# Token columns of the projection matmuls: 512 + 512 + 128 instead of three times 384

## The reference

```
xn = rms_norm(x)
q, k, v, o, ig, fg, glu, xq, gates = split(xn @ w_in)
y_ml = mLSTM(q, k, v, ig, fg) * sigmoid(o)
y_cv = silu(layer_norm(causal_dwconv(ga * sigmoid(gb))))
y_xa = mem_attention(xq, mk, mv)
mixed = sum over b of sigmoid(gates[b]) * (y_b @ w_branch[b])
x = x + rms_norm(mixed @ w_out)
x = x + rms_norm((silu(fa) * fb) @ w_ffn_out)     # fa, fb from rms_norm(x) @ w_ffn_in
```

## Time and profile before

| | |
|---|---|
| median of three runs | 2942.29 us |
| span of the profiled execution | 2940.9 us |
| TensorE busy | 2737.7 us (93%), 15764 matmuls |
| weight loads busy | 2676.4 us (91%) |
| VectorE, GpSimd, ScalarE busy | 1066.5, 1043.4, 791.7 us |
| mean granted TensorE clock | 0.970 |
| projection units | 80, from about 130 to 1140 us |
| branch units | 24, in three groups |

### The profile page before, as it was taken

The page is one execution under the profiler, slowest core; times in us unless marked ns, Lnnn a source line. Parts: engine busy times, 40 slices in busy tenths (PEclk is TensorE's granted clock), DMA queues, the critical chain, the costliest instruction groups (busy, mean ns, idle before and its releaser), DMA issues.

```text
span 2940.9 us, 41651 instructions
## 1 busy us (share of the span) xinstructions
PE 2737.7 (93%) x15764; PEld 2676.4 (91%) x15764; DVE 1066.5 (36%) x1418; ACT 791.7 (27%) x1172; POOL 1043.4 (35%) x525
## 2 busy tenths in 40 slices
PE   5899999999999998989988989779998899969997
PEld 5899999999999998978788879769997899969997
DVE  3320399999922222156433423231103211041101
ACT  4321111111113323044311410233333333233332
POOL 5411222222211112122011201346665566646664
PEclk9999999999999999999999989989999899989999
DMA  6422333433252232534654435424444244433442
GB/s 174 139 88 92 121 118 112 136 115 108 91 178 89 82 96 100 168 106 117 210 174 167 148 133 187 156 76 123 137 141 136 86 121 139 132 115 114 124 134 78
DMA packets 469265, 372.11 MB, mean 127 GB/s; under 512 B 13626, under 2 KB 437906, under 8 KB 469168
## 3 DMA queue, kind: packets, MB, share of 16 engines
q1 hardware_dynamic: 454264, 317.52, 35.7%
q10 hardware_dynamic: 14912, 53.48, 4.7%
HBM read 285.86 MB, written 85.55 MB: 126 GB/s over the span
## 4 chain that ended last, share of the span: by engine, by line
issue 47%; PE 34%; POOL 14%; DVE 2%; ACT 1%; POOLq 1%; DMA 1%; SPq 0%; DVEq 0%; ACTq 0%
PE PS L274 29%; POOL w_lo L266 12%; PE PS L1504 1%; PE PS L1523 1%; PE PS L1179 1%; PE PS L1187 1%; PE PS L1145 1%; POOL m_lo L1776 1%; DVE x_T L549 0%; POOL m_lo L1987 0%; PE PS L1152 0%; DMA stage<-in_state_conv 0%; DVE y_T L1342 0%; POOL n_r L1971 0%; PE PS L1140 0%
## 5 line engine op out<-in xcount | busy, mean ns | idle before, releaser
L266 POOL TENSOR_TENSOR w_lo<-w_raw,w_hi 128x1024 fp32r<-128x1024 f32 (+1 forms) x324 | 838.1, 2588 | 1434.0 <-ACT w_hi L262 1433.9
L262 ACT CAST w_hi<-w_raw 128x1024 fp32r<-128x1024 f32 (+1 forms) x324 | 356.0, 1099 | 1755.5 <-PE PS L274 1749.0
L274 PE MATMUL PS<-A_hi,w_hi 128*128 128x384 f32 x3024 | 752.4, 336 | 19.0 <-DVE A_lo L948 10.0
L274 PE MATMUL PS<-A_lo,w_hi 128*128 128x384 f32 x3024 | 747.8, 335 | 0.0
L274 PE MATMUL PS<-A_hi,w_lo 128*128 128x384 f32 x3024 | 747.4, 335 | 0.0
L274 PEld LDWEIGHTS PS<-A_hi,w_hi 128*128 128x128 f32 x3024 | 546.2, 189 | 22.9 <-issue 18.0
L274 PEld LDWEIGHTS PS<-A_lo,w_hi 128*128 128x128 f32 x3024 | 546.2, 188 | 0.0
L274 PEld LDWEIGHTS PS<-A_hi,w_lo 128*128 128x128 f32 x3024 | 545.8, 188 | 0.0
L274 PE MATMUL PS<-m_hi,w_hi 128*128 128x384 f32 x1248 | 428.1, 343 | 28.1 <-DVE m_lo L1776 14.9
L274 PE MATMUL PS<-m_lo,w_hi 128*128 128x384 f32 x1248 | 425.7, 341 | 0.0
L274 PE MATMUL PS<-m_hi,w_lo 128*128 128x384 f32 x1248 | 425.4, 341 | 0.0
(11 more groups left out here) (265 smaller groups left out, 2103.5 us busy)
## 6 DMA issues: line engine op xcount, KB each, us to landing
w_raw<-in_w_ffn_in SPq DMA_DIRECT2D x132, 512.0 KB, 3.8
proj_d<-stage ACTq DMA_DIRECT2D x80, 576.0 KB, 2.8
w_raw<-in_w_in SPq DMA_DIRECT2D x80, 512.0 KB, 4.0
w_raw<-in_w_ffn_out SPq DMA_DIRECT2D x48, 704.0 KB, 4.6
gate_in<-proj_d SPq DMA_DIRECT2D x24, 576.0 KB, 6.2
part_d<-part_out SPq DMA_DIRECT2D x24, 576.0 KB, 4.5
w_raw<-in_w_branch SPq DMA_DIRECT2D x24, 512.0 KB, 4.2
w_raw<-in_w_out SPq DMA_DIRECT2D x24, 512.0 KB, 4.0
```

The lines of the kernel that those rows point to most:

```text
L262: nc.scalar.copy(w_hi[:, s % SPLIT, 0:kt], w_raw[:, s, 0:kt]).then_inc(w_hi_done, 1)
L266: nc.gpsimd.tensor_tensor(w_lo[:, s % SPLIT, 0:kt], w_raw[:, s, 0:kt], w_hi[:, s % SPLIT, 0:kt].bitcast(F32), ALU.subtract).then_inc(w_lo_ ...
L274: last = nc.tensor.matmul(out, w[:, k], m(k, c), start=start and k == 0 and n == 0, stop=stop and k == kt - 1 and n == 2)
```

## The change

The 1152 token columns of a unit go as 512, 512 and 128 columns instead of three times 384. The first two pieces fill a bank each, the third takes a quarter of one. As the pieces now lie without a gap across the three banks, the instructions that read them see one row of 1152 (`bank_rows`) instead of three pieces. In the first branch unit the waits for the low parts follow the new pieces: piece 0 (tokens 0 to 511) needs the first and the middle third, pieces 1 and 2 need all three. The FFN, the layer norm and the output projection keep their thirds of 384.

```diff
-                    nc.scalar.activation(thirds(stage[:, s % 2]), PS[:, 3 * (s % 2):3 * (s % 2) + 3, 0:TC], func,
+                    nc.scalar.activation(stage[:, s % 2], bank_rows(s % 2), func,
                                          scale=scale).then_inc(p_copied, 1)
...
         def a_hi(k, c):
-            return A_hi[:, k, TC * c:TC * (c + 1)]
+            return A_hi[:, k, 512 * c:min(512 * (c + 1), NTOK)]
 
         def a_lo(k, c):
-            return A_lo[:, k, TC * c:TC * (c + 1)]
+            return A_lo[:, k, 512 * c:min(512 * (c + 1), NTOK)]
 
         def banks(b):
-            return [PS[:, 3 * b + c, 0:TC] for c in range(3)]
+            return [PS[:, 3 * b], PS[:, 3 * b + 1], PS[:, 3 * b + 2, 0:NTOK - 1024]]
+
+        def bank_rows(b, p=slice(0, P)):
+            return PS[p, 3 * b:3 * b + 3].rearrange("p n c -> p (n c)")[:, 0:NTOK]
...
-            steps.mark(nc.vector.tensor_scalar(thirds(g_i[:]), PS[0:H, 3:6, 0:TC], g_bias[0:H, 0:1], None, ALU.add))
+            steps.mark(nc.vector.tensor_scalar(g_i[:], bank_rows(1, slice(0, H)), g_bias[0:H, 0:1], None, ALU.add))
...
                         for c in range(3):
-                            pe.wait_ge((ln_lo, ln_lo_pool, ln_lo)[c], (1, 1, 2)[c])
+                            pe.wait_ge(ln_lo, 1 if c == 0 else 2)
+                            pe.wait_ge(ln_lo_pool, 1)
...
-                    nc.vector.scalar_tensor_tensor(out=thirds(part_out[:, s % 2]), in0=thirds(gate_in[:, s % 2]), scalar=1.0,
-                                                   in1=PS[:, 3 * (s % 2):3 * (s % 2) + 3, 0:TC], op0=ALU.add,
+                    nc.vector.scalar_tensor_tensor(out=part_out[:, s % 2], in0=gate_in[:, s % 2], scalar=1.0,
+                                                   in1=bank_rows(s % 2), op0=ALU.add,
                                                    op1=ALU.mult).then_inc(part_mul if n else part_done, 1)
```

More of the change, by code:

```diff
@@ L829, in dve_proj @@
             dve.wait_ge(wif_used, 1)
-            steps.mark(nc.vector.tensor_scalar(thirds(g_i[:]), PS[0:H, 3:6, 0:TC], g_bias[0:H, 0:1], None, ALU.add))
-            nc.vector.tensor_scalar(thirds(g_f[:]), PS[32:32 + H, 3:6, 0:TC], g_bias[32:32 + H, 0:1], None, ALU.add).then_inc(gate_read, 1)
+            steps.mark(nc.vector.tensor_scalar(g_i[:], bank_rows(1, slice(0, H)), g_bias[0:H, 0:1], None, ALU.add))
+            nc.vector.tensor_scalar(g_f[:], bank_rows(1, slice(32, 32 + H)), g_bias[32:32 + H, 0:1], None, ALU.add).then_inc(gate_read, 1)
             dve.wait_ge(gate_read, 1)
```

## The result

The changed kernel takes 3092.7 us (median of 4 runs, 3087.1 to 3094.6) against 2942.5; the ratio is 1.0505, 95% interval 1.0491 to 1.0518. It is 5% slower. The forecast was 3100 us, within 3010 to 3140.

A forecast was written before the change was run, and what follows sets the result against it. TensorE was taken as the bound, busy for 93% of the span. 2520 triples at +60.0 ns (151.2 us) plus 6.6 us for the later branch start give +157.8 us on 2942.3: 3100 us, range 3010 to 3140.

The forecast's parts named there:

- The count and the place: Projection, branch and gate products: 2520 triples (three matmuls passing 1152 tokens by one weight piece), +60.0 ns each on TensorE, +151.2 us.
- The 128-column matmul: Third piece of a triple: its columns end before the next weights can load, so 113.3 ns; bounds 57.8 and 223.
- The 512-column matmul: First two pieces: 233.3 ns, stepping 60.0 ns per 128 columns from 256 (113.3) and 384 (173.3); bounds 216 and 240.
- (a): Smaller extra per 512: 226.7 ns with constant 13.3 ns, 3067 us (chance 0.22); or 216 ns, 3013 us (0.10).
- the unit of 13.9 us: Projection: ScalarE's evacuations, one per unit of 72 matmuls, would stand 13.9 us apart instead of 12.48.
- a 128 that is followed after less than 100 ns: In a triple: the next matmul starting under 100 ns after the 128 would make the prediction wrong; 113 expected.
- The start of the branch product: First branch matmul also waits for GpSimd's third of the low parts: start moves from 1149.23 to about 1155.8, +6.6 us.
- (b): Faster: next weights load ahead of the 128's start, 128 costs 57.8 ns, 512 costs 216; 2877 us, chance 0.05.
- (c): No change: matmuls cost by columns alone, triple stays 520.0 ns, only the later branch start counts; 2949 us, chance 0.04.
- (d): 128-column matmul falls into a slow form, 223 ns instead of 113.3; 3377 us, chance 0.06.
- (e): Pauses after each 128 lower the granted clock from 1.00 to 0.93 in the projection; 3210 us, chance 0.03.
- The formula from the Trainium skill: Warm matmuls take columns over 2.4 GHz plus 2.5 ns; triple 487.5 ns, so the change would gain, nearly as (b).

The follow-up runs named there:

- half_weights: Changed kernel, but the first 512-token matmul uses only 64 of 128 weight columns, so only the load after the 128-column matmul is shorter: 2938.8 us, 0.9984 of the kernel before.
- before_half_weights: Kernel before (three times 384) with 64 of the 128 weight columns on all three pieces in projection and branch units: 2946.2 us, 1.0008 of the kernel before.
- four_pieces: Pieces of 320 + 320 + 256 + 256 columns (first product of a unit: one 512 for the last two) instead of three times 384: 2976.8 us, 1.0112.
- wait_only: Kernel before (three times 384) with only the changed kernel's two wait lines in the first branch unit: 2949.4 us, 1.0024 of the kernel before.

## Why the prediction was right

**The count and the place**: 2520 triples, all on TensorE. (577 - 520) x 2520 + 6.6 = 150 us against 149.4 measured. The stage of the FFN kept its work: TensorE is busy for 1053.36 us in the last 1150 us of the span, 1053.64 before.

**The 128-column matmul**: taken at 113.3 ns, measured at 111 in a row and 108 in a triple, from load to load: 0.06 us to the listed start of the next 512 and some 0.05 of waiting. That the wait is the load's is shown by half_weights (gone with a load half as long) and before_half_weights (no effect where nothing is exposed). The exposed part is about 50 ns a triple, beside a loss of 57 against three times 384. (The 0.1115 us of a plain float32 matmul of 128 columns is 0.1117 by its row; nothing hangs on it.)

**The 512-column matmul**: taken at 233.3 ns by going on with 60 ns for each 128 columns. In a row it is 226.6, so the constant addition of rival (a) was right there; in the triple the two take 236 and 233. The result agrees, the argument doesn't hold. By its step 320 columns should take 143 ns, and they take 147 to 150; four_pieces should take 513 ns and takes 533, which the constant gives. The step came from the 113.3 ns of 256 columns; in the experiments a 256 takes 117 to 124, and the trace of the kernel before has another pace as well, in 4 of the 16 units of the memory tokens:

```profile
107.80 0.28 PE L274 MATMUL PS<-mem_hi,w_lo 128*128 128x256 f32 x1
...
110.27 0.28 PE L274 MATMUL PS<-mem_hi,w_lo 128*128 128x256 f32 x1
```

These are 21 periods, 117.6 ns each, at the same granted clock of 1.00 as in the stretch of the earlier trace rows; the step from them would have been 56 ns. So the mechanism of the 128 was right, and that the 512 had the right size in this mixture is luck. The forecast's 157.8 us are more than the measured 149.4 because the 128 was put 5 ns too high and the two 512s together 2 ns too low, and because the units from 56 on take 573 ns a triple.

**The signs**: the unit of 13.9 us came out (13.85), and so did the load that starts with the 128. The listed starts did not. They lie 0.28, 0.23 and 0.06 us apart, not 233, 233 and 113 ns, and by its letter the sign "a 128 that is followed after less than 100 ns" spoke against the prediction. The sign took the listed start for the beginning of the columns; read from load to load, the three are 236, 233 and 108 ns.

**The start of the branch product**: +6.6 us forecast, 6.66 in the trace (16.63 after 9.97), 6.5 by wait_only.

**The rivals**: (b) would need the load to begin ahead of the 128; it begins with it, at 400.87. (c) and (d) fall with the 108 to 111 ns, (e) with the granted clock of 1.00. The formula from the Trainium skill, "TensorE: Matmul & The Clock Gate", section "Back-to-back issue gap", gave an estimate of 487.5 ns a triple; the section itself offers it for a single matmul by itself and says that it counts too little for short ones in a stream of weight loads and matmuls, which the prediction did not say. The trace does not agree with the formula: 226.6 ns for a 512 in a row instead of 215.8, and 111 for a 128 instead of 55.8.

**What stays open**: why a 512 takes 4 to 10 ns more beside shorter pieces than in a row (0 to 3 at the faster level of half_weights), which is most of what uneven splits cost; why the 256-column matmuls of the memory tokens have two paces, 113.3 and 117.6 ns; and why the triple of half_weights takes 527 ns in the loop of units 12 to 55 and 513 before and after it. All are differences of a few ns in how matmuls of this kind follow each other; the runs show them and not their cause.

## What to carry to other kernels

Where every matmul loads its own weights, a tail piece is not priced by its columns: it costs at least one load (108 to 111 ns for 128 columns of these weights), and the rest of the load stands in front of the next matmul. Each matmul also brought some 13 ns of its own here, so more pieces lose as well. Of the splits tried, three equal pieces, each longer than a load, were the fastest; full banks gained nothing. Price a size from more than one stretch of the trace: one pace of 256 columns, where there were two, misled the prediction's step. To see such a wait, compare the listed duration of the matmul after the short one with that of its kind, or read the distance from load to load; the list of waits doesn't have it.

## What was not expected of the hardware

Shortening one load in three to half made the triple of 512 + 512 + 128 take 513 ns outside the loop of units 12 to 55, less than the 520 of three times 384, although its load count and columns are the same. And a 256-column matmul put in place of the 128 cost 9.5 ns more a triple, not 1 to 4.
